# An order of its own for the last three steps of a software-pipelined projection loop

## What is computed

```python
h = rms_norm(x, g_attn);  proj = h @ w_in            # 1376 columns, cut among the head groups
# A: sliding-window attention, 8 query heads, 2 key heads, window of 2 chunks of 64, sinks, rotary
# B: latent attention, 4 heads: low-rank q and kv, rotary tail, chunk-causal mask over all frames
# M: attention of 4 heads over 256 memory tokens
mixed = concat([out_a, out_b, out_m])                # 512 + 256 + 256
x = x + mixed @ w_o
x = x + square(relu(rms_norm(x, g_ffn) @ w_ff1)) @ w_ff2
```

## Time and profile before

| What | Value |
|---|---|
| median of 3 runs | 2208.3 us (2207.64 to 2211.73) |
| the profiled execution | 2209.09 us, of which the span from first to last instruction 2207.3 us |
| mean granted TensorE clock | 0.989 of full |
| TensorE busy | 2135.6 us, 97% of the span |
| VectorE, GpSimd, ScalarE busy | 1444.0 us (65%), 1092.9 us (50%), 1035.4 us (47%) |
| step 15's third cut ends, front's last matmul starts | about 392.2 us, 450.33 us |
| first matmul of attention starts | 455.42 us |
| TensorE's longest wait in those last steps | 4.96 us, on VectorE |

### The profile page before, as it was taken

One profiled execution on the slowest core, in us unless ns is written; L12 is line 12 of the kernel. 1 busy time (PEld: TensorE's weight loads), 2 busy tenths in 40 slices (PEclk: granted clock), 3 DMA queues, 4 the chain that ended last, 5 costly groups with the idle time before them and its releaser, 6 DMA issues. The chain is left out here.

```text
span 2207.3 us, 31733 instructions
## 1 busy us (share of the span) xinstructions
PE 2135.6 (97%) x10024; PEld 1760.3 (80%) x10024; DVE 1444.0 (65%) x2095; ACT 1035.4 (47%) x1863; POOL 1092.9 (50%) x898
## 2 busy tenths in 40 slices
PE   8999999879999999979999989999999999999999
PEld 7899999757777677768888878888888888888887
DVE  5788888868665655468776697776644565354463
ACT  6566666547666666653333344333423323223221
POOL 2665665734465566637656666656445720020220
PEclk9999999889999999999999999999999999999999
DMA  6142242678557665575444575444577762233363
GB/s 240 41 117 81 82 117 63 202 217 252 177 174 210 188 187 160 180 253 176 165 149 143 169 243 176 144 150 146 193 245 274 245 214 105 96 133 134 136 224 117
DMA packets 291403, 370.64 MB, mean 168 GB/s; under 512 B 27280, under 2 KB 186192, under 8 KB 289488
## 3 DMA queue, kind: packets, MB, share of 16 engines
q1 hardware_dynamic: 291280, 369.08, 51.6%
HBM read 244.07 MB, written 124.93 MB: 167 GB/s over the span
## 5 line engine op out<-in xcount | busy, mean ns | idle before, releaser
L128 PE MATMUL bank<-f_t_hi,f_w_hi 128*128 128x512 f32 x896 | 349.9, 391 | 6.7 <-issue 4.4
L128 PE MATMUL bank<-f_t_lo,f_w_hi 128*128 128x512 f32 x896 | 349.0, 389 | 0.0
L128 PE MATMUL bank<-f_t_hi,f_w_lo 128*128 128x512 f32 x896 | 348.9, 389 | 0.0
L128 PE MATMUL bank<-f_w_hi,f_a_hi 128*128 128x512 f32 x896 | 348.5, 389 | 0.0
L128 PE MATMUL bank<-f_w_lo,f_a_hi 128*128 128x512 f32 x896 | 348.5, 389 | 0.0
L128 PE MATMUL bank<-f_w_hi,f_a_lo 128*128 128x512 f32 x896 | 348.5, 389 | 0.0
L2331 POOL TENSOR_TENSOR a_p_lo<-a_prob,a_p_hi 128x512 fp32r<-128x512 f32 (+1 forms) x192 | 234.1, 1228 | 196.5 <-DVE a_p_hi L2472 94.6
L1778 DVE TENSOR_TENSOR f_a_lo<-f_a_raw,f_a_hi 128x1024 fp32r<-128x1024 f32 x112 | 160.3, 1431 | 71.4 <-ACT f_a_hi L1705 71.2
L128 PEld LDWEIGHTS bank<-f_t_hi,f_w_hi 128*128 128x128 f32 x896 | 168.4, 188 | 44.2 <-issue 8.8
L1680 POOL TENSOR_TENSOR f_r<-f_r,f_y 128x512 f32<-128x512 f32 x24 | 42.0, 1786 | 324.5 <-DMA f_r<-s_x 324.5
L128 PEld LDWEIGHTS bank<-f_t_hi,f_w_lo 128*128 128x128 f32 x896 | 168.4, 188 | 34.9
(11 more groups left out here) (323 smaller groups left out, 4876.6 us busy)
## 6 DMA issues: line engine op xcount, KB each, us to landing
f_a_raw<-s_aop SPq DMA_DIRECT2D x112, 512.0 KB, 4.3
w_raw<-in_w_ff SPq DMA_DIRECT2D x64, 512.0 KB, 5.3
s_aop<-f_a SPq DMA_DIRECT2D x128, 256.0 KB, 4.3
s_aop<-f_s SPq DMA_DIRECT2D x96, 256.0 KB, 2.4
f_w_raw<-in_w_ff SPq DMA_DIRECT2D x64, 256.0 KB, 5.4
f_t_raw<-s_hop SPq DMA_DIRECT2D x14, 1024.0 KB, 8.6
f_r<-in_w_ff SPq DMA_DIRECT2D x48, 256.0 KB, 6.0
a_vals<-s_v SPq DMA_DIRECT2D x40, 264.0 KB, 4.9
```

The source lines that it names most:

```text
L128: ins = pe.matmul(out, a, b, start=(first and j == 0), stop=(last and j == n - 1))
```

## The change

Four parts.

- **Steps 16 to 18.** `steps` ends with step 15 and then calls a function `drain(ta, tb, tc)` of each engine for tiles 13, 14 and 15. The bodies of the steps were cut into small functions (`score`, `weigh`, `row_tops`, `rotate_heads`, `store_v` and so on), and each engine's `drain` calls them in an order of its own, with the pieces of the early visits between them. Visit 0 is done differently: first the matmuls with `w_hi` of both halves (`first_highs`, 16), later the eight with `w_lo` (`first_lows`) in the order 2, 0, 3, 1 of its pieces. VectorE makes `w_lo` 0 alone, GpSimd 2, 3 and 1 in that order.
- **Step 15.** The loads of `w_o` and `swa` go from the end to the beginning of SyncE's step. TensorE turns the heads of tile 14 before the third cut of tile 15, its latents before the cut's last eighth, the keys behind it; ScalarE and VectorE split them in that order, VectorE ahead of the latents' norm, ScalarE ahead of its copy of the third cut.
- **Buffers and banks.** Tile 15's latents go to buffers of their own (`last_hi`, `last_lo`, in the place of `proj`), and its second latents, its latent transposes and its memory queries to other parts of the PSUM banks (`pG`, the upper half of `pB`).
- **Attention's constants.** `neg_max` comes first and VectorE waits for it alone, at its first negation; ScalarE waits for all ten at its first exponent.

```diff
@@ steps @@
-            for s in range(NT - 4, NT + 3):
+            for s in range(NT - 4, NT):
                 body(0, s)
+            drain(*(tile_at(0, n) for n in range(NT - 3, NT)))
@@ SyncE @@
+                def drain(ta, tb, tc):
+                    E["load_swa"](sp, 2)
+                    for v in (0, 2, 3, 1):
+                        E["load_x"](sp, v)
+                    store_mix(ta)
+                    load_tab_l(tc)
...
+                    first_loads(sp, R, S)
+                    store_l(ta, l_hi, l_lo)
+                    E["load_swa"](sp, 3)
+                    store_v(tb)
+                    store_m(tc)
+                    E["store"](sp, 0)
+                    store_mix(tb)
...
+                    E["store"](sp, 3)
@@ GpSimd @@
+                def drain(ta, tb, tc):
+                    n = Chain(pool, n_pool, tc.n, N_POOL)
+                    head_roots(tc, n)
+                    E["split_w_lo"](pool, 2)
+                    head_gains(tc, n)
+                    E["split_w_lo"](pool, 3)
+                    scale_probs(tb)
+                    E["split_w_lo"](pool, 1)
+                    E["split_m_lo"](pool, 1)
+                    split_values(tc)
...
@@ ScalarE @@
+                def drain(ta, tb, tc):
+                    prob_high(ta)
+                    ac.wait_ge(projected, NT * B_PE)
+                    E["split_w_hi"](ac)
+                    E["split_m_hi"](ac, 0)
+                    scale_latents(tc, 2)
+                    l = Chain(ac, l_act, tb.n, L_ACT)
+                    exponent(tb)
+                    take_up(tb, l)
+                    take_values(tb, l)
+                    take_out(ta)
...
+                    take_values(tc, l)
+                    take_out(tb)
+                    for j, src in enumerate((pC, pD)):
+                        wait(ac, l_stored[j], 32 * tb.n)
+                        latent_high(tb, j, src, l_hi)
...
@@ VectorE @@
+                def drain(ta, tb, tc):
...
+                    prob_low(ta)
+                    w = Chain(dve, w_dve, tb.n, W_DVE)
+                    row_tops(tb, w)
+                    norm_heads(tc, n)
+                    E["split_m_lo"](dve, 0)
+                    E["split_w_lo"](dve, 0)
+                    rotate_heads(tc, n)
+                    prob_sums(tb, w)
+                    rotate_latents(ta)
...
+                    E["add"](dve, y_bank[1], 2, 1)
+                    prob_low(tc)
...
@@ TensorE @@
+                def drain(ta, tb, tc):
+                    score(tb)
+                    weigh(ta)
+                    turn_mem(tc, pB[:, 256:512])
+                    pe.wait_ge(n_act, NT * N_ACT)
+                    E["first_highs"](pe, y_bank)
...
+                    turn_keys(tc)
+                    E["first_lows"](pe, y_bank)
...
+                    turn_latents(ta, 0, pC)
...
+                    turn_probs(tb)
+                    wait(pe, m_lo_done, tc.n + 1)
+                    score(tc)
+                    E["half"](pe, y_bank[0], 1, 0)
+                    weigh(tb)
+                    E["half"](pe, y_bank[1], 1, 1)
...
@@ attention, GpSimd @@
+        pool.memset(neg_max[:, :, :], 0.0).then_inc(const_made, 1)
...
-        pool.memset(neg_max[:, :, :], 0.0).then_inc(const_made, 1)
@@ attention, VectorE @@
+            if U == 0:
+                dve.wait_ge(const_made, 1)
...
-        dve.wait_ge(const_made, 10)
```

885 lines of the change are left out of this document (520 added, 365 removed).

## The result

| | kernel before | changed kernel |
|---|---|---|
| median | 2208.6 us (4 runs, 2207.64 to 2211.73) | 2221.14 us (4 runs, 2220.45 to 2225.07) |
| ratio, 95% interval | | 1.0058 (1.0046 to 1.007): slower |
| profiled execution | 2209.09 us, span 2207.3 | 2220.55 us, span 2218.8 |
| granted TensorE clock | 0.989 | 0.987 |

Slower, as forecast, but by 12.5 us where I had said 6.6, and above my range (2218.5). To see where the spans' 11.5 us lie I use three marks: VectorE's rest of tile 15's turned `x` (the last row ahead of the changed steps), the barrier (GpSimd's and ScalarE's first instruction of attention) and attention's first maxima.

A forecast was written before the change was run, and what follows sets the result against it. TensorE, busy 97%, gains only where it waits or runs slowly; the barrier's opening decides. Barrier +8.4 and constants -1.8 give +6.6 us, a median of 2214.9 us; range 2201 to 2218.5.

The forecast's parts named there:

- the walk's sum: Front's last steps, followed operation by operation: last add at 461.4, barrier at 463.5 us, 8.4 later than before.
- The signs that I had listed: Trace checks: tile 14's score near 395, last w_o rest 419 to 421, first load near 422, barrier 461 to 465.
- Each us after 420.2 is a us of the end: Last rest of w_o, taken as ready at 420.2 us: each microsecond later delays the end by one.
- the floor of the store: Tile 15's values, written by ScalarE, must wait until tile 14's values are stored, at 442.3 us; before, written at 434.66.
- SyncE's queue, which decides: Before the barrier: tile 14's values go out behind 21 attention loads, at 437.2, and that store sets the end.
- The 2.07 us that lie now between the last add and the barrier: End of the front: the kernel before's 2.07 us stays, taking the last add at 461.4 to the barrier at 463.5.
- The constants: Attention's start: first maxima no longer wait for GpSimd's last memset; 1.8 us gained, bounds 0 and 1.9.
- Tile 15's own buffers and banks: End of the front: ScalarE's wait for tile 14's stores goes; worth 0 to 1 us before, 0 in the new order.
- The faster rival: Transfers come in time: barrier at 452.2, with the constants -4.7 us, 2203.6 us; chance 0.2.
- holds: Last steps: VectorE operations with two SBUF inputs and GpSimd's two-input ones run in turn; last w_o rest 420.2, without 415.
- I charge nothing: TensorE's clock may fall twice, not once; slowed matmuls end in the same waits, so 0 (3 us without waits).

The follow-up runs named there:

- rest_early: waits_back with GpSimd making the last rest of w_o (part 1) ahead of its scaling of tile 14's probabilities; 2222.0 us, ratio 1.0059 to the kernel before.
- rotary13_early: waits_back with VectorE's rotary of tile 13's latents ahead of its rest of w_o's part 0; 2220.5 us, ratio 1.0052 to the kernel before.
- constants_alone: The kernel before with only the change's reordering of attention's constants and the waits for them; 2207.0 us, ratio 0.9987.
- loads_last: waits_back with the engines' orders changed in several places and SyncE's stores and mixed-rows load ahead of attention's 21 loads; 2207.1 us, ratio 0.9986 to the kernel before.
- waits_back: The changed kernel with TensorE's loop waits ahead of the latent, head and probability transposes in their old order; 2219.7 us, ratio 1.0045 to the kernel before.
- rotary14_early: waits_back with VectorE's rotary of tile 14's latents and sums of tile 15 ahead of tile 1's second add; 2217.3 us, ratio 1.0038 to the kernel before.
- out_first: waits_back with ScalarE taking out tile 15's mixed rows ahead of tile 15's last two latents; 2217.3 us, ratio 1.0036 to the kernel before.
- waits_moved: The kernel before with only those TensorE loop waits in the changed kernel's order (lat_made last); 2211.3 us, ratio 1.0008.

## Why the prediction was right or wrong

**Direction and the walk's sum.** Slower was right, and from the mark to the barrier I had +8.4 against +8.96 measured. Taken from the changed kernel's rows less the 2.14 us, every station was within 2 us of where I had it, and nearly all of them sooner: `score` of tile 14 at 394.7 (said 394.8), the last rest of w_o ready at 418.2 (420.2), the first load at 420.5 (421.6), the last load's issue over at 432.3 (434.3), tile 14's values issued at 435.4 (437.2), tile 15's written at 440.8 (442.3), weighing at 452.0 (453.1), the last add over at 460.4 (461.4). The signs that I had listed came out on one scale or the other (the last rest ends at 420.4 by the profile's time, inside my 419 to 421), but for the barrier, at 466.2 where I had 461 to 465, and the maxima, 0.8 behind it and not 1.1. My list of TensorE's waits left out the 2.85 us at 410.44; the walk had its successor, some 5 us for ScalarE, and 4.85 came.

**"The bodies were cut into small functions" at no cost.** The step that failed outright is one that I did not write down. I costed the last steps and step 15, and took the loop's body for unchanged. It was not: `lat_made` moved from the first of three waits to the last, two other pairs changed places with it, and six passes through the hardware loop cost 1.6 us, shown in both directions. The two kernels' texts show the moved wait side by side, and I gave it no price.

**"Each us after 420.2 is a us of the end."** Wrong. rest_early brought the last rest 6.2 us sooner and the barrier 0.1. VectorE's rotary of tile 13, held by the same GpSimd work, was due at the same time, and adds, latent rests and the half clock behind it. I had charged that rotary 1.4 us, shared with the rest; it took 6.1. So tile 15's `score` came at 427.5 on my scale, inside my 424.5 to 429, and its place cost nothing, since the floor of the store and VectorE's order lay behind it.

**"SyncE's queue, which decides."** Half right. The floor was real and well placed, and rotary13_early ran into it for 5.55 us. But it did not decide alone: VectorE's order (the rotary of tile 14 behind `add(1,1)`) held TensorE to 443.8 as well, and taking away the store by itself was worth 0.5 us. A walk that takes the latest of several arrivals gives the right end and the wrong handle. What I missed of the queue is its second grip: tile 13's latents' stores, which bind as soon as the values don't.

**"The 2.07 us that lie now between the last add and the barrier."** Mis-sized by 1.56: SyncE's last six issues, not the add, came last. Against it, VectorE's and TensorE's last stations were each some 1 us sooner than I had them. That the sum came out in spite of it is luck.

**The constants.** -1.8 forecast, -2.2 measured at the first maxima in the changed kernel, -2.9 (-0.9 to -4.9) in the median of constants_alone. Right in kind and place. That all of it stays to the end, as my sum had it, isn't shown: constants_alone's profile gives 1.9 back later.

**Tile 15's own buffers and banks.** ScalarE's copies into them wait for TensorE alone, as said, and stood ahead of tile 15's mixed rows, which cost the 1.56 us above. No run has these buffers alone, nor step 15's part of the change, nor gives VectorE its second rest of w_o back; what each of these is worth isn't shown.

**The faster rival.** "If holds cost nothing" and the values land in time, barrier at 452.2. loads_last comes close to it by another way, 453.1 on the same scale (85.93 behind the mark at 367.16), with holds left in (tile 13's rotary takes 5.8 us there in place of 1.4). So the queue and the orders around it were price enough to lose by, and the holds alone need not lose; what they still cost there no run shows.

**The clock.** "I charge nothing" for the second fall fits this path, I think only by the floor behind it; no run tests that. Behind the barrier one profiled execution lost 2.6 us, mostly to longer low stretches; on average over the profiles 1.5 us of the constants' gain stay.

**The sum.** 8.96 - 2.21 is 6.75, against my 6.6. In the profiled pair the 4.7 us above it are the order of waits (1.6), an opening 0.5 later and the stretch behind the maxima (2.6, low clock for the most part), of which the last two are scatter of single executions. They can't explain the medians, which differ by 12.5 us. Of the 5.9 us by which these exceed my 6.6 the runs show 1.6, the order of waits; about 4 stay open. waits_back, without the 1.6, is still 9.8 us above the kernel before by the medians. A candidate is the further fall of the clock that the profiles of rotary13_early, rotary14_early and out_first show, up to 3.0 us in one of them; whether the changed kernel's other executions had it, no trace shows. The range left no room for terms outside the stretch that I had looked at.

## What to carry to other kernels

Compare the issue orders of two versions over the whole program, also where the change is said to be a mere rewriting; a reordered wait in a loop body is paid on every pass. When several arrivals fall within a microsecond or two of each other, the latest gives the time, but moving it gains nothing: look for edits that move all of them, and try them together before dropping one. In a queue that only issues transfers, put every store that frees a buffer ahead of prefetches for the next phase, and look at what it issues last before a barrier: here 21 loads of 0.4 to 0.6 us of issue each, needed only behind the barrier, held the buffers of two tensors, and moving them was worth 8.4 us to the barrier (4.8 in the medians) once the engines' own orders were in shape, and 0.3 before.

## What the runs showed of the hardware that I had not expected

- On TensorE the new order of the waits ahead of the latents' and heads' transposes cost 0.28 us more on each pass of the loop, though no wait of the profile stands there (waits_back and waits_moved). The cause stays open.
- The barrier opened 1.71 to 1.72 us behind the end of SyncE's last issue in all fifteen profiles, whether the last add ended 0.02 us or 1.3 us ahead of that issue's start.
- Several short operations of VectorE in a row can each be held by one of GpSimd: a 128x256 product of 0.42 us took 2.44, and four operations of 1.4 us together took 6.1.
- The opening of the kernel, up to tile 3, came 0.2 to 3 us later in other executions than in the kernel before's profile, and stayed so to the end of the loop: a shift at one mark says nothing until one has seen where it grows.
- With the same code behind the barrier, the time there varied from 1748.1 to 1753.3 us between profiles.
